# Six pieces of the adaLN modulation moved from an attention stage to the seam between two layers

## The reference, cut to what matters

```
mod_l = split(silu(c)     @ ada_w[l] + ada_b[l], 6)     # ada_w[l]: 1024 x 6144
mod_c = split(silu(c_ctx) @ ada_w[l] + ada_b[l], 6)
h = modulate(rms_norm(x, norm1), mod[0], mod[1])
x = x + mod[2] * mixers(h)                   # neighbourhood attention, MLA, GLA, merged, projected
x = x + mod[5] * experts(modulate(rms_norm(x, norm2), mod[3], mod[4]))
```

## Time and profile before

| | |
|---|---|
| median of 3 runs | 2627.26 us (2625.07 to 2627.48) |
| the profiled execution | 2627.82 us, span 2626.0 us |
| busy: PE, PE weight loads | 2468.0 us (94%), 1553.5 us (59%) |
| busy: DVE, ACT, POOL | 999.3, 667.3, 110.7 us |
| mean granted TensorE clock | 0.978 |

### The profile page before, as it was taken

One profiled execution on the slowest core, in us unless ns is written; L12 is line 12 of the kernel. 1 busy time (PEld: TensorE's weight loads), 2 busy tenths in 40 slices (PEclk: granted clock), 3 DMA queues, 4 the chain that ended last, 5 costly groups with the idle time before them and its releaser, 6 DMA issues. The chain is left out here.

```text
span 2626.0 us, 40702 instructions
## 1 busy us (share of the span) xinstructions
PE 2468.0 (94%) x17398; PEld 1553.5 (59%) x17398; DVE 999.3 (38%) x2235; ACT 667.3 (25%) x1356; POOL 110.7 (4%) x161
## 2 busy tenths in 40 slices
PE   5999999999899899999999999998998999999998
PEld 3888877778686434343434588876676643333432
DVE  4545354344774312121211464455348421111113
ACT  3621232322633102011111362243236311010101
POOL 1000100000000101000000000100000000000000
PEclk9999999999999699999999999999999999999999
DMA  6111466151553899999999312322217379999996
GB/s 218 57 49 33 136 203 204 49 180 45 192 181 107 316 406 399 383 393 362 390 366 393 95 57 65 81 69 73 73 58 230 135 279 409 409 409 409 409 409 272
DMA packets 244771, 591.20 MB, mean 225 GB/s; under 512 B 11846, under 2 KB 120624, under 8 KB 243568
## 3 DMA queue, kind: packets, MB, share of 16 engines
q1 hardware_dynamic: 233312, 554.41, 56.0%
q0 software_dynamic: 11280, 34.19, 4.6%
HBM read 558.08 MB, written 30.47 MB: 224 GB/s over the span
## 5 line engine op out<-in xcount | busy, mean ns | idle before, releaser
L1066 PE MATMUL ps<-h_hi,m_lo 128*128 128x512 f32 (+1 forms) x1152 | 345.6, 371 | 2.0 <-DVE arena L2238 1.7
L1505 PE MATMUL ps<-arena 128*32 128x512 f32 x1740 | 260.7, 600 | 1.3 <-DVE arena L2477 1.3
L1506 PE MATMUL ps<-arena 128*32 128x512 f32 x588 | 260.2, 600 | 0.0
L1039 PE MATMUL ps<-m_lo,h_hi 128*128 128x256 f32 (+1 forms) x1248 | 234.4, 290 | 5.1 <-DVE m_lo L2211 3.0
L1066 PEld LDWEIGHTS ps<-h_hi,m_lo 128*128 128x128 f32 x1152 | 207.8, 190 | 52.0 <-issue 13.8
L1039 PEld LDWEIGHTS ps<-m_lo,h_hi 128*128 128x128 f32 x1248 | 197.1, 195 | 13.7 <-issue 9.7
L1066 PE MATMUL ps<-h_lo,m_lo 128*128 128x512 f32 (+1 forms) x576 | 204.8, 356 | 0.0
L1617 PE MATMUL ps<-arena 128*64 128x512 f32 x832 | 187.8, 597 | 12.3 <-DMA arena<-in_moe_w_up 9.6
L1039 PE MATMUL ps<-m_lo,h_lo 128*128 128x256 f32 (+1 forms) x624 | 177.7, 285 | 0.0
L1505 PEld LDWEIGHTS ps<-arena 128*32 128x32 f32 x1740 | 71.6, 111 | 170.0 <-issue 167.9
L1039 PE MATMUL ps<-h_hi,m_lo 128*128 128x512 f32 (+1 forms) x512 | 141.8, 354 | 8.3 <-DVE h_lo L2316 7.5
(11 more groups left out here) (391 smaller groups left out, 4426.3 us busy)
## 6 DMA issues: line engine op xcount, KB each, us to landing
arena<-in_moe_w_up SPq DMA_DIRECT2D x101, 1024.0 KB, 13.9
arena<-in_moe_w_gate SPq DMA_DIRECT2D x100, 1024.0 KB, 14.6
arena<-in_moe_w_down SPq DMA_DIRECT2D x100, 1024.0 KB, 15.0
ring<-in_w_in SPq DMA_DIRECT2D x42, 1024.0 KB, 5.3
arena<-in_ada_w SPq DMA_DIRECT2D x37, 1024.0 KB, 5.5
oT<-in_moe_w_up SPq DMA_DIRECT2D x27, 1024.0 KB, 14.9
oT<-in_moe_w_down SPq DMA_DIRECT2D x24, 1024.0 KB, 12.8
oT<-in_moe_w_gate SPq DMA_DIRECT2D x16, 1024.0 KB, 12.1
```

The source lines that it names most:

```text
L1039: last = mm(to, stationary, moving, start=at == 0 and k == 0, stop=at == 2 and k == KD - 1)
L1066: last = mm(to, w[:, k, cols], h[:, k, seg], start=n == 0 and k == 0, stop=n == 2 and k == KD - 1)
L1505: mm(ps[r][32 * b:32 * b + 32, :], c_xg[:, k, j, 32 * b:32 * b + 32], w, start=k == 0, stop=k == KD - 1)
L1506: last = mm(ps[r][96:128, :], c_xg[:, k, j, 32 * r:32 * r + 32], up[:, kk, 512:1024], start=k == 0, stop=k == KD - 1)
```

## The change

- `ADA`: the MLA attention keeps one piece of seven (h = 28). The routing's 13 are now h = 29 to 41. A new stage `edge` has the last six, h = 42 to 47.
- SP loads these six behind the last expert weights of layer 0, each into the slot that comes next in the ring of 11 (`edge_slot`, `late_home`, `late_there`), and waits for `p_used` as a weight load does. The landing counts of layer 1 are raised accordingly, and the sixth tile of x is counted on `x_kept`.
- PE does the six pieces (`late_products`) in the place of the 7 fillers behind layer 0's last expert. The 24 fillers at layer 1's start become 9.
- ACT copies and keeps the six pieces' rows ahead of the squares, and then takes a square root of a constant, 128 x 1, nobody's input, which brings the table load there.
- Behind `modulate(l)`, in both layers, ACT takes an exponential of a constant in the same way.

```diff
--- before.py
+++ after.py
@@ -335,7 +335,7 @@
 
 
 
-        ADA = {"first": 8, "na": 20, "mla": 7, "route": 13}
+        ADA = {"first": 8, "na": 20, "mla": 1, "route": 13, "edge": 6}
         UNITS_AHEAD, LOADS_AHEAD = 2, 5
 
         def ada_first(stage):
@@ -370,7 +370,7 @@
 
         def ada_zeroed(h):
 
-            return 1 + sum(h >= ada_first(stage) for stage in list(ADA)[1:])
+            return 1 + sum(h >= ada_first(stage) for stage in ("na", "mla", "route"))
 
         def late_sums(h):
 
@@ -380,11 +380,20 @@
 
         def late_home(h):
 
+            if h >= ada_first("edge"):
+                slot = edge_slot(h)
+                return carve(ar, 8 * slot, KD, 256) if slot < PAIR_SLOTS else carve(oTf, 8 * (slot - PAIR_SLOTS), KD, 256)
             i = h - ada_first("route")
             return carve(hTf, 8 * i, KD, 256) if i < 3 else carve(ar, 8 * LATE_SLOTS[i - 3], KD, 256)
 
+        def edge_slot(h):
+
+            return (TURNS * PER_TURN + h - ada_first("edge")) % SLOTS_OF[0]
+
         def late_there(h):
 
+            if h >= ada_first("edge"):
+                return pair_in[edge_slot(h)], 16 * (slot_landings(DEPTH - 1, edge_slot(h)) - (1 if edge_slot(h) < NT - 1 else 0))
             i = h - ada_first("route")
             if i < 3:
                 return w_in[i], 48 * slot_count(0, KD - 1, W_SLOTS) + 16
@@ -617,12 +626,13 @@
 
         def x_back(ti):
 
-            return pair_in[ti], 16 * slot_landings(DEPTH - 1, ti)
+            return (pair_in[ti], 16 * slot_landings(DEPTH - 1, ti)) if ti < NT - 1 else (x_kept, 16 * NT + 16)
 
         def slot_landings(l, slot):
 
             loads = sum(len(range(slot, TURNS * PER_TURN, slots)) for slots in SLOTS_OF[:l] if slot < slots)
-            return loads + max(1, LATE_SLOTS.count(slot)) + (1 if l and slot < NT else 0)
+            late = l * [edge_slot(h) for h in ada_late("edge")].count(slot)
+            return loads + max(1, LATE_SLOTS.count(slot)) + late + (1 if l and slot < NT - 1 else 0)
 
         def slot_count(l, j, slots):
 
@@ -873,6 +883,9 @@
                     sp.dma_start(xn2_spill[t * P:(t + 1) * P, :], xn2[:, t, :]).then_inc(xn2_out, 16)
                 for g in range(0, TURNS):
                     pair_loads(l, g)
+                for i, h in enumerate(ada_late("edge") if l == 0 else ()):
+                    sp.wait_ge(p_used, before("p_used", l) + PAIR_SLOTS + TURNS * PER_TURN + i + 1 - SLOTS_OF[l])
+                    late_load(h)
             for ti in range(SEQ // P):
                 sp.wait_ge(fin_ok, ti + 1)
                 sp.dma_start(out[0][ti * P:(ti + 1) * P, :], fin[:, ti, :]).then_inc(stored, 16)
@@ -1083,7 +1096,7 @@
                     last.then_inc(hc_up, 1)
 
                 if l:
-                    kept_running(ps[0], 24)
+                    kept_running(ps[0], 9)
                 pe.wait_ge(xn_ok, sum(NORMS[:s + 1]))
                 turned(0)
                 turned(1)
@@ -1472,7 +1485,7 @@
                         late_turned(h - 1)
                     late_turned(ada_late("route")[-1])
                     kept_running(ps[5], 3)
-                    pe.wait_ge(ada_raw, 48)
+                    pe.wait_ge(ada_raw, ada_first("edge"))
                 else:
                     kept_running(ps[6], 15)
                 pe.wait_ge(top_ok, before("top_ok", l) + 1)
@@ -1593,7 +1606,9 @@
                 for g in range(1, TURNS - 1):
                     turn(g, False, False)
                 turn(TURNS - 1, False, True)
-                kept_running(ps[0], 7)
+                pe.wait_ge(ye_ok, before("ye_ok", l + 1) - 2)
+                late_products(ada_late("edge"))
+                pe.wait_ge(ada_raw, 48)
 
             def experts_paired(l):
                 nq = 2 * NQ[l]
@@ -2181,6 +2196,7 @@
                     late_rows(ada_late("route")[1:3])
                     late_kept(ada_late("route")[2])
                 modulate(l)
+                do(st[:, 62:63], ones[:, 0:1], ACT.Exp)
                 if l == 0:
                     late_copied(ada_late("route")[3])
                     late_rows(ada_late("route")[4:5])
@@ -2191,6 +2207,11 @@
                     late_kept(ada_late("route")[-1])
 
                 (grouped if l < DEPTH - 1 else paired)(l)
+                if l < DEPTH - 1:
+                    late_copied(ada_late("edge")[0])
+                    late_rows(ada_late("edge")[1:])
+                    late_kept(ada_late("edge")[-1])
+                    do(st[:, 63:64], ones[:, 0:1], ACT.Sqrt)
                 scattered_rows_squared(l, xn1 if l < DEPTH - 1 else fin)
```

## The result

| | before | after |
|---|---|---|
| median of 10 runs each, on one chip | 2622.53 us (2617.25 to 2628.26) | 2609.24 us (2601.79 to 2615.42) |
| ratio, with its 95% interval | | 0.9945 (0.9926 to 0.9965) |
| the profiled execution | 2627.82 us | 2604.41 us, span 2602.6 us |
| mean granted TensorE clock | 0.978 | 0.982 |

What follows compares the result with a forecast made beforehand. PE was taken as the bound in the MLA attention and routing, fillers then DVE in the seam; -8.7 - 0.8 - 3.1 = -12.6 us gave 2614.7 us (forecast 2611 to 2617, wider range 2608.5 to 2621).

Steps and rivals of the forecast that it cites:

- Part 1: Layer 0's MLA attention: six pieces leave units 3 to 8, where PE is the bound; -8.7 us.
- Part 2: Layer 0's routing: exponential's table loaded earlier, behind the modulation, so the exponential, pieces and end come earlier; -0.8 us.
- Part 3: Seam between the layers: pieces replace fillers, PE's transposes come earlier, then DVE's low part is last; -3.1 us.
- R3: MLA attention doesn't get shorter, because the chain of maxima and exponentials becomes the bound; 2623.4 us, chance 0.07.
- (b): Layer 0's routing: PE sets the end, with eight pieces at clock 0.50 until 880.00; starting them earlier moves the end equally.
- R2: Layer 0's routing: shorter idle time keeps the clock at 2.4 GHz; 12.6 us beyond the forecast, 2602 us, chance 0.08.
- R1, heavy: Seam: clock falls to 1.2 GHz when the pieces begin, 2.96 us each; 2621.2 us, chance 0.05.
- Loads first ... Cost 0: Seam: six 1 MB loads ahead of layer 1's chunk loads land 5.5 us after issue, all by 1456; cost 0.
- R4: Seam: the pieces' weights land late and delay layer 1's opening; slower, 2639 us if the last piece ends at 1500; chance 0.03.
- the 22 that the prediction gave as a sign: Seam: layer 1's transposes come 22 us behind the last expert product, not 26.8, if the forecast is right.
- The squares' 0.66: Seam: without the table load among ACT's squares, the sixth square starts 0.66 us earlier; bounds 0 and 1.28.
- R1, light: Seam: clock falls to 1.2 GHz in idle time behind nine fillers; 1 to 3 us lost, 2615.7 to 2617.7, chance 0.14.

Runs made afterwards that it cites:

- routing fillers: Two fillers ahead of PE's wait for layer 0's normalised affinities: added to after, 2603.59 us, ratio 0.9928; added to before, 2617.75 us, ratio 0.9973.
- the second chunk is moved: After with two fillers ahead of layer 0's affinities wait, and layer 1's second chunk load issued behind the x loads: 2602.21 us, ratio 0.9921.

## Why the prediction came out as it did

| step | forecast | measured |
|---|---|---|
| Part 1, six pieces leave the MLA attention | -8.7 | -8.4 |
| Part 2, the exponential's table | -0.8 | -0.85 (the exponential alone, in before) |
| Part 3, the seam | -3.1 | 0.0 and -1.0 (two profiles of after), -1.6 and -2.0 (with routing fillers); -3.1 once the second chunk is moved |
| the sum | -12.6 | parts as read -9.3 to -11.3; times -13.3 between the medians, -13.2 to -14.2 with the routing fillers in both |
| the time | 2614.7 | 2609.24; the upper group of after is at 2612.6 to 2615.4 |

**Part 1 was right**, and R3 wrong: PE is not idle in the attention without the pieces either.

**Part 2 was right** in size. That ACT has nothing better to do there is seen too: it waits 0.92 us behind the preload in the trace of the exponential alone.

**The step that failed for the time is (b)**, "then does eight pieces at a granted clock of 0.50, until 880.00", taken as the way the kernel runs. It is one of two ways: about half of all executions of before are 10 us faster (15 of 29 on one chip, 2615.5 to 2619.7, against 14 of 2625.7 to 2628.4). R2 named the place and the price, but as something that the change might bring, by a clock that never falls; the clock does fall in after too, and comes back behind the first piece. R2 had it that "the gap is only a quarter shorter" speaks against it, and gave 0.08. The runs show that the gap's length between 2.16 and 3.00 us does not decide it: with either length both ways occur, with 2.16 us in the very same program. So after's upper group lies at the forecast (2613.9 in its middle, for 2614.7), its lower group at R2's 2602, and a median of ten falls between them by how many of each there are. The Trainium skill (TensorE: Matmul & The Clock Gate, section "Why this matters for your kernels"), by which an idle gap between bursts puts the clock back to half, speaks of the fall. The traces of this place agree with it, though the section warns of gaps longer than the 2.15 us that were enough here: the clock fell in that gap or up to 1.4 us behind it in all six profiles with 2.15 to 3.00 us of idle time, and in none of the seven with a filler there. What the two groups hang on is when it comes back. The six profiles show something to follow up: in the three where it came back behind the first piece, it had fallen between 0.7 us before and 0.3 us behind the start of the affinities' transposes; in the three where it stayed down, 1.1 us before them, or 0.4 and 1.4 us behind. How the fall lies against the pieces may decide it; no run was made to test that.

(In R1, heavy, the 2.96 us a piece hold PE's wait for ACT's last copy, 0.69 us, and the way to the fillers; the pieces at 1.2 GHz start 2.77 us apart.)

**The step that failed for the size is Part 3's "Loads first ... Cost 0".** The prediction asked when the pieces' weights land, and R4 priced their being late for PE. They weren't: no piece waits for a DMA, although such a load takes 12.4 or 13.3 us to land in after (medians of the two triples), for the 5.5 of the earlier trace rows. The sixth landed at 1445.9, 11.6 us later than "all six by 1456" would have it (1434.3 by after's clock) and 4 us before PE began its products. That 5.5 is the median of pieces loaded in other stages; the page of before has the loads of the same size that stand ahead in this queue at nearly three times that (the last five of them, behind which the queue empties, at 8.7):

```profile
arena<-in_moe_w_down SPq DMA_DIRECT2D x100, 1024.0 KB, 15.0
```

The prediction didn't ask what stands behind them in SP's queue. It said that the chunk loads "wait for a later event anyway"; true, but they then start when the queue is through, at 1435.37 (before's 1453.56, moved by the 21.7 us that the experts end earlier, would be 1431.9), take 10.36 us to issue instead of 2.18, and lie beside the scatter-add. That costs 1.75 and 2.1 us in the two profiles of after (7.41 and 7.76 us from the scatter-add to the x load, against 5.5 to 5.7 in the eight profiles where the chunk loads ahead of the scatter-add have landed by 2.6 us behind its issue), and 1.0 in the three with the routing fillers and both chunks ahead (6.6). The longer the last chunk load runs on beside it, the longer it takes. Where that load lands 1.9 to 2.6 us behind the scatter-add's issue, the scatter-add takes 5.5 to 5.6 us; where it lands at 4.7 to 4.9, 6.6; at 6.2, 7.4; at 8.3, 7.8. PE's transposes came 25.6 us behind the last expert, not the 22 that the prediction gave as a sign; 2.1 of the difference are the scatter-add's. By the Trainium skill (DMA: Bandwidth & Descriptors, section "Queues, rings and completion order") a DMA engine takes its queues in turn, a packet at a time; the trace agrees in so far as the scatter-add, on a queue of its own, is drawn out by 2 us in after and there not held until the last chunk load is through, which lands 0.5 us behind its end; in the four other such profiles the scatter-add ends 1.2 to 1.9 us behind that landing, which tells neither way.

**The squares' 0.66 was 0 to 0.3 us** in the two profiles that bear on it. A bound of zero was named. In before the fifth tile of x landed 7.9 us behind its issue, at 1483.1, and its square stands at 1483.17: the squares were already waiting for their tiles, and the last tile did not land at the 1483.7 that the prediction let it. Without the early root, in the kernel with routing fillers, the load cost 0.3. Where tiles land sooner it can cost more; the profile of the exponential alone has 0.8.

**R1, light, happened in its mechanism**: the clock falls in the 7.46 us of idle time ahead of layer 1's transposes (0.57). Its price of 1 to 3 us is not shown: the modulated rows wait for DVE at either clock (2.90 us behind the transposes), and the way to the attention takes 234.62 us in after and 232.50 with routing fillers and the same fall, 230.7 to 235.9 in all six profiles with a fall there, and 230.6 to 234.9 in the seven without.

**What stays open.** The parts that were read sum to 9.3 to 11.3 us, the times to 13.2 to 14.2. That 13.3 came out so near to 12.6 is therefore in part luck: a part that gave 0 to 1 us of its 3.1 was made up by something that nobody forecast. The rest lies in the experts of layer 0 and in layer 1, where the change does next to nothing. From the modulated rows to the end it takes 1127.5 to 1136.1 us in the thirteen profiles, with short falls of the clock in other places each time, and this scatter is larger than the rest that is to be explained. A part of it may be a shift of the kernel against these falls; no run here shows that.

## What to carry to other kernels

Run the kernel before more than three times and sort the times before reading its profile: a profile is one draw, and if the times have two groups the first question is which one it is of and in which stretch they differ. Two fillers in a gap of 3 us ahead of a long row of small products were worth half as much in before as the whole change, and halved the spread; fewer fillers in the seam gave all that the change was to give there. When loads are added to an in-order queue, price what is queued behind them against the transfers that it will now lie beside, above all a latency-bound one at the head of a chain, not only the new loads against their own reader.

## What was not expected of the hardware

- The same program, with the same 2.16 us of idle time, had 2.4 GHz back behind the first of the pieces in one execution and only in the fillers behind the last in the other; 10.6 us hang on it.
- Six 1 MB loads in a row behind the expert weights took SP 19.3 us to issue and 12.4 or 13.3 us (medians of the two triples) to land, where 5.5 was the median of such loads in the other stages of before; the three chunk loads behind them took 10.36 us to issue, for 2.18.
- The last scatter-add took 5.5 to 5.7 us from issue to the next load when the chunk loads ahead of it had landed within 2.6 us of its issue, and 6.6 to 7.8 when they ran on beside it for 4.7 us or more (DMA share 0.57 and 0.81 over these stretches, before and after).
